# A decoder layer on one core: the products of the U tiles joined in pairs, VectorE adding the halves, table copies on ScalarE, 84 candidate sums

## What is computed

```
qry = (xt @ w_q).reshape(N, HEADS, 2, 128)
s = einsum('nhpd,pkd->nhpk', qry, sub_keys)         # 8 heads, 2 halves, 128 keys
s_top, i_top = top_k(s, 16)
cand = s_top[:, :, 0, :, None] + s_top[:, :, 1, None, :]    # 16 x 16 sums
cand_id = i_top[:, :, 0, :, None] * 128 + i_top[:, :, 1, None, :]
best, pos = top_k(cand, 16)
expert, gate = cand_id at pos, softmax(best)
hid = gelu(einsum('cd,chkd->chk', x, u_tab[expert]))
y = einsum('chk,chkd->cd', gate * hid, v_tab[expert])
```

## Time and profile before

| | |
|---|---|
| median of 3 runs | 1098.83 us (1098.72 to 1099.35) |
| the profiled execution's own time | 1099.08 us |
| its span, first to last instruction | 1097.3 us |
| mean granted TensorE clock | 0.997 |
| DVE, ACT, POOL busy | 70%, 51%, 16% of the span |

### The profile page before, as it was taken

How to read it: one execution, slowest core, us unless ns; L and a number is a source line. 1 busy time by engine, 2 the same in 40 slices (tenths; PEclk the granted TensorE clock), 3 DMA queues, 4 the chain that set the end, 5 groups by cost and what they waited for, 6 DMA issues and landing times.

```text
span 1097.3 us, 19861 instructions
## 1 busy us (share of the span) xinstructions
PE 1081.6 (99%) x6760; PEld 969.3 (88%) x6760; DVE 773.4 (70%) x1403; ACT 559.2 (51%) x903; POOL 177.5 (16%) x118
## 2 busy tenths in 40 slices
PE   8999999999999999999999999999999999999996
PEld 6888888678999999999999999998888888888885
DVE  4457657387999868889998777765555555555556
ACT  4347544564344555555556545545554455455553
POOL 2040002203000002223334555520000000000001
PEclk9999999999999999999999999999999999999998
DMA  7554344253445554444444443445565655555553
GB/s 280 190 194 155 134 157 150 96 173 129 159 166 180 185 179 155 156 163 160 153 154 153 142 146 134 137 153 193 198 208 204 205 193 191 191 191 191 192 193 112
DMA packets 52711, 186.48 MB, mean 170 GB/s; under 512 B 6320, under 2 KB 6704, under 8 KB 52672
## 3 DMA queue, kind: packets, MB, share of 16 engines
q1 hardware_dynamic: 50864, 181.30, 48.7%
q0 software_dynamic: 944, 3.15, 0.8%
q10 hardware_dynamic: 864, 1.57, 0.4%
HBM read 184.94 MB, written 1.05 MB: 169 GB/s over the span
## 4 chain that ended last, share of the span: by engine, by line
PE 92%; DVE 3%; DMA 2%; ACT 2%; POOL 1%; issue 1%; POOLq 0%; SPq 0%; DVEq 0%; ACTq 0%
PE ps L1172 17%; PE ps L1174 17%; PE ps L1173 17%; PE ps L1499 10%; PE ps L1500 10%; PE ps L1501 10%; PE ps L1460 5%; DMA raw<-w_tiles_in 1%; PE ps L1224 1%; ACT whi L462 1%; DVE wlo L726 1%; PE ps L1426 1%; PE ps L1300 1%; PE ps L1311 0%; PE ps L1316 0%
## 5 line engine op out<-in xcount | busy, mean ns | idle before, releaser
L726 DVE TENSOR_TENSOR wlo<-raw,whi 128x1024 fp32r<-128x1024 f32 x341 | 421.4, 1237 | 258.7 <-ACT whi L462 256.6
L462 ACT ACTIVATE whi<-raw 128x1024 fp32r<-128x1024 f32 x343 | 363.2, 1060 | 303.9 <-DMA raw<-w_tiles_v 167.8
L1172 PE MATMUL ps<-ahi,whi 128*128 128x256 f32 x1152 | 332.5, 289 | 0.4 <-DVE alo L987 0.4
L1174 PE MATMUL ps<-ahi,wlo 128*128 128x256 f32 x1152 | 325.8, 283 | 0.0
L1173 PE MATMUL ps<-alo,whi 128*128 128x256 f32 x1152 | 325.7, 283 | 0.0
L1172 PEld LDWEIGHTS ps<-ahi,whi 128*128 128x128 f32 x1152 | 220.6, 191 | 0.6 <-issue 0.6
L1173 PEld LDWEIGHTS ps<-alo,whi 128*128 128x128 f32 x1152 | 220.8, 192 | 0.0
L1174 PEld LDWEIGHTS ps<-ahi,wlo 128*128 128x128 f32 x1152 | 220.5, 191 | 0.0
L1499 PE MATMUL ps<-whi,hhi 128*128 128x512 f32 x512 | 199.3, 389 | 0.9 <-DVE wlo L726 0.9
L1500 PE MATMUL ps<-wlo,hhi 128*128 128x512 f32 x512 | 199.2, 389 | 0.0
L1501 PE MATMUL ps<-whi,hlo 128*128 128x512 f32 x512 | 199.2, 389 | 0.0
(11 more groups left out here) (198 smaller groups left out, 922.8 us busy)
## 6 DMA issues: line engine op xcount, KB each, us to landing
raw<-w_tiles_u SPq DMA_DIRECT2D x128, 512.0 KB, 3.2
raw<-w_tiles_v SPq DMA_DIRECT2D x128, 512.0 KB, 3.2
raw<-w_tiles_in SPq DMA_DIRECT2D x63, 512.0 KB, 3.2
raw<-w_tiles_q SPq DMA_DIRECT2D x16, 512.0 KB, 3.2
raw<-w_tiles_out SPq DMA_DIRECT2D x8, 512.0 KB, 3.2
xraw<-xT ACTq DMA_DIRECT2D x4, 256.0 KB, 6.3
xt<-x POOLq DMA_DIRECT2D x1, 1024.0 KB, 7.8
raw<-w_tiles_in SPq DMA_DIRECT2D x2, 256.0 KB, 4.6
```

Of the source, the lines that this page charges most:

```text
L462: act.activation(whi[:, tile.slot, :], raw[:, tile.slot, :], ACT.Copy)\
L726: dve.tensor_tensor(wlo[:, tile.slot, :], raw[:, tile.slot, :], whi[:, tile.slot, :].bitcast(F32), ALU.subtract)\
L1172: pe.matmul(out, ah, bh, start=start, stop=False)
L1174: return pe.matmul(out, al, bh, start=False, stop=stop)
```

## The change

- `ahi` and `alo` become two views of one tensor `pair`, in which high and low activations of a slice lie side by side. In U tiles 1 to 127 `by_pairs` takes the place of `by_tokens`: one product of 512 columns (high weights times high and low activations) and one of 256 columns (low weights times high activations, added to the second half of the bank). A tile has 16 products in place of 24, and the hidden values are the sum of the two halves of a bank.
- ACT copies the second half of the bank to SBUF (`low`), DVE adds it to the first half in PSUM (`add_low`), and ACT's gelu waits for that sum (`summed`). The late tokens' gelu is written back to PSUM, which takes the place of `gelu_late`. A bank is given back to PE at `merged`, from tile 38 on, in place of `hid_used`.
- The copy of a table to rows of `H` moves from DVE to ACT (`copy_g`, behind `split_hi`), and `into_h` keeps the multiplication, one iteration later. `hots` stands before `merge`, `widen_i` before gelu.
- `routing` makes 84 candidate sums in place of 256: rank a of one half meets only the first 16, 8 or 4 ranks of the other (`PAIR_ROWS`). The step that takes positions apart becomes two, with eight small operations more. Small tensors of the routing lie in unused rows of `H`.

```diff
+    pair = place("pair", [P, KC, 2, SEQ], F32R)
+    ahi, alo = pair[:, :, 0, :], pair[:, :, 1, :]
...
+        def copy_g(c):
+            there = after(c) + 1
+            act.wait_ge(S["g_done"], c + 1)
+            act.activation(H[:, there:NK, c * BLK:(c + 1) * BLK], tables(c)[:, there:NK, :], ACT.Copy)\
+                .then_inc(S["g_copied"], 1)
...
             act.wait_ge(S["tiles_used"], T_U + u + 1)
+            if u > 0:
+                if u > NTMP:
+                    act.wait_ge(S["summed"], u - NTMP)
+                act.activation(low[:, u % NTMP, :], ps[:, HID[u % 4], SEQ:2 * SEQ], ACT.Copy).then_inc(S["low_ready"], 1)
+            c = CHUNK_AFTER.get(u + 1)
+            if c is not None:
+                widen_i(c)
+            if u > 0:
+                act.wait_ge(S["summed"], u)
             if late > 0:
-                if u - FIRST_LATE >= NTMP:
-                    act.wait_ge(S["merged"], u - FIRST_LATE - NTMP + 1)
-                last = act.activation(gelu_late[:, u % NTMP, 0:late], ps[:, HID[u % 4], 0:late], ACT.Gelu)
+                last = act.activation(ps[:, HID[u % 4], 0:late], ps[:, HID[u % 4], 0:late], ACT.Gelu)
             if late < SEQ:
                 last = act.activation(H[:, u, late:SEQ], ps[:, HID[u % 4], late:SEQ], ACT.Gelu)
             last.then_inc(S["hid_used"], 1)
-            c = CHUNK_AFTER.get(u + 1)
-            if c is not None:
-                widen_i(c)
             split_hi(Tile(T_U + u + AHEAD))
+            c = CHUNK_AFTER.get(u)
+            if c is not None:
+                copy_g(c)
...
-                own.do(dve.tensor_tensor(cand[:, :, :], top[:, 0, :, None].to_broadcast([P, TOPK, TOPK]),
-                                         top[:, 1, None, :].to_broadcast([P, TOPK, TOPK]), ALU.add))
+                for first, end, width in PAIR_ROWS:
...
+                    own.step(dve.tensor_tensor(pairs, top[:, 0, first:end, None].to_broadcast([P, rows, width]),
+                                               top[:, 1, None, 0:width].to_broadcast([P, rows, width]), ALU.add))
...
+        def add_low(u):
+            hidden = ps[:, HID[u % 4], 0:SEQ]
+            dve.wait_ge(S["low_ready"], u)
+            dve.tensor_tensor(hidden, hidden, low[:, u % NTMP, :], ALU.add).then_inc(S["summed"], 1)
...
         for u in range(TILES_U):
+            if u > 0:
+                add_low(u)
+            c = CHUNK_AFTER.get(u + 2)
+            if c is not None:
+                hots(c)
             if u >= FIRST_LATE:
                 merge(u)
-            c = CHUNK_AFTER.get(u)
+            c = CHUNK_AFTER.get(u - 1)
             if c is not None:
                 into_h(c)
...
+        def by_pairs(tile, bank):
+            tile_ready(tile)
+            for k in range(KC):
+                cols = slice(k * P, (k + 1) * P)
+                pe.matmul(ps[:, bank, :], whi[:, tile.slot, cols], pair[:, k, :, :].rearrange("p a n -> p (a n)"),
+                          start=k == 0, stop=False)
+                last = pe.matmul(ps[:, bank, SEQ:2 * SEQ], wlo[:, tile.slot, cols], ahi[:, k, :], start=False,
+                                 stop=k == KC - 1)
+            last.then_inc(S["tiles_used"], 1)
```

More of the change, by code:

```diff
@@ L43 @@
 PH, NK, TOPK = 8, 128, 16
+PAIR_ROWS = ((0, 1, 16), (1, 3, 8), (3, 16, 4))
+PAIRS = sum((end - first) * width for first, end, width in PAIR_ROWS)
 ALPHA = 2.0 ** 0.25
@@ L277, in layer @@
     iota16 = place("iota16", [P, TOPK], BF16)
[L278 to L281, removed]
+    low = place("low", [P, NTMP, SEQ])
+    cand = place("cand", [P, PAIRS], alias=work_at + 99 * row + row // 2)
+    top = place("top", [P, 2, TOPK], alias=work_at + 99 * row + row // 2 + 352)
+    hot16 = place("hot16", [P, 4, 2, 2 * P], BF16, alias=work_at + 100 * row)
+    rank = place("rank", [P, 2, 2, 2, P], BF16, alias=work_at + 100 * row)
     gsum = place("gsum", [P, PH])
@@ L291, in layer, with tables @@
     HID = (2, 3, 4, 5)
+    def tables(c):
+        return ps[:, RING[c % 2], :].rearrange("p (n i) -> p i n", i=NK)
     Y_BANKS = (4, 5, 2, 3)
@@ L673, in _ @@
             last.then_inc(S["hid_used"], 1)
-            c = CHUNK_AFTER.get(u + 1)
+            split_hi(Tile(T_U + u + AHEAD))
+            c = CHUNK_AFTER.get(u)
             if c is not None:
-                widen_i(c)
-            split_hi(Tile(T_U + u + AHEAD))
+                copy_g(c)
             for t in range(NT):
@@ L1021, in routing @@
                     own.step(dve_idx(ids[:, a, 8:16], top[:, a, 8:16], s[a]))
-                own.do(dve.tensor_tensor(cand[:, :, :], top[:, 0, :, None].to_broadcast([P, TOPK, TOPK]),
-                                         top[:, 1, None, :].to_broadcast([P, TOPK, TOPK]), ALU.add))
+                at_pair = 0
+                for first, end, width in PAIR_ROWS:
+                    rows = end - first
+                    pairs = cand[:, at_pair:at_pair + rows * width].rearrange("p (a b) -> p a b", b=width)
+                    own.step(dve.tensor_tensor(pairs, top[:, 0, first:end, None].to_broadcast([P, rows, width]),
+                                               top[:, 1, None, 0:width].to_broadcast([P, rows, width]), ALU.add))
+                    at_pair += rows * width
+                own.wait()
                 yield
@@ L1034, in routing @@
             own.step(dve.tensor_copy(topf[:, 1, :].rearrange("p (q n) -> p q n", q=2), topi[:, :, 1, :]))
-            own.step(dve.tensor_scalar(posab[:, 0, 1, :], which, 4, None, ALU.logical_shift_right))
-            own.do(dve.tensor_scalar(posab[:, 1, 1, :], which, TOPK - 1, None, ALU.bitwise_and))
-            own.step(dve.tensor_copy(posf[:, 1, :].rearrange("p (a n) -> p a n", a=2), posab[:, :, 1, :]))
+            own.step(dve.tensor_scalar(posab[:, 0, 1, :], which, 2, None, ALU.logical_shift_right))
+            own.do(dve.tensor_scalar(posab[:, 1, 1, :], which, P - 1, None, ALU.bitwise_and))
+            own.do(dve.tensor_copy(posf[:, 1, :].rearrange("p (a n) -> p a n", a=2), posab[:, :, 1, :]))
+            yield
+            unit, place_in = posf[:, 1, 0:P], posf[:, 1, P:2 * P]
+            past4, past, over, twice = (rank[:, n // 2, 1, n % 2, :] for n in range(4))
+            own.step(dve.tensor_scalar(past4, unit, 4.0, None, ALU.is_ge))
+            own.do(dve.tensor_scalar(over, unit, 8.0, 0.0, ALU.subtract, ALU.max))
+            own.do(dve.scalar_tensor_tensor(out=past, in0=unit, scalar=6.0, in1=past4, op0=ALU.is_ge, op1=ALU.add))
+            own.do(dve.scalar_tensor_tensor(out=past, in0=unit, scalar=8.0, in1=past, op0=ALU.is_ge, op1=ALU.add))
+            own.step(dve.tensor_tensor(unit, past, over, ALU.add))
+            own.do(dve.tensor_tensor(twice, past, past4, ALU.add))
+            own.do(dve.scalar_tensor_tensor(out=twice, in0=twice, scalar=2.0, in1=over, op0=ALU.mult, op1=ALU.add))
+            own.do(dve.scalar_tensor_tensor(out=place_in, in0=twice, scalar=-4.0, in1=place_in, op0=ALU.mult,
+                                            op1=ALU.add))
             own.do(dve.tensor_tensor(gdiff[:, 1, :].rearrange("p (h k) -> p h k", k=TOPK), vals,
@@ L1474, in _ @@
         for k in range(1, 4):
-            by_tokens(Tile(T_U + k), HID[k])
+            by_pairs(Tile(T_U + k), HID[k])
         hidden(4, SEL_AT[0] + 1)
@@ L1478, in _ @@
         hidden(SEL_AT[0] + 1, ONE_PER_TWO)
-        for k in range(4):
+        for k in range(8):
             m = ONE_PER_TWO + k
-            pe.wait_ge(S["hid_used"], m - 3)
-            by_tokens(Tile(T_U + m), HID[k])
+            if m >= FIRST_LATE + 4:
+                pe.wait_ge(S["merged"], m - 3 - FIRST_LATE)
+            else:
+                pe.wait_ge(S["hid_used"], m - 3)
+            by_pairs(Tile(T_U + m), HID[k % 4])
             if k == 0:
```

45 lines of the change are left out of this document (22 added, 23 removed).

## The result

The changed kernel takes 1175.87 us (median of 6 runs, 1175.51 to 1177.1), the kernel before, run beside it, 1099.01. The ratio is 1.070, with a 95% interval of 1.069 to 1.071: slower by 77 us. The forecast was 1169 us, within 1148 to 1198.

A forecast was written before the change was run, and what follows sets the result against it. The prediction took PE's spacing in the U tiles to bound the kernel before, and a serial DVE-ACT loop the changed one: +32.5 + 8.5 + 33.0 - 4.3 = +69.7 on 1099.1 gives 1169 us, range 1148 to 1198.

The forecast's parts named there:

- The closed round: U tiles: sum, gelu, `split_hi`, `split_lo`, routing step and next sum run serially through DVE and ACT; chance 0.69.
- Its length: One round through DVE and ACT without a routing step: 2.96 us, or 3.01 with gelu in two pieces, above PE's 2.77.
- the mis-sized term: Tiles 34 to 87: rounds, routing steps, exponential and gates take 212.5 us against 179.5 before, +33.0.
- comparison steps beside POOL's multiplications as a danger: Rival of a longer loop: slow PSUM operations or stretched comparison steps; 0.3 us more a round gives 1194, 0.5 gives 1211; chance 0.12.
- The routing steps: DVE steps now paid inside the round: head steps 0.90 us in the mean, comparison steps 1.15, two decoding steps about 2.9.
- `hots`, `merge`, `into_h`, the copies at nothing: Tiles 34 to 87: these table operations cost nothing; uncovered, the first three would add up to a microsecond a tile.
- the cover that the prediction named: DVE's waiting time beside gelu and `split_hi`, 0.03 + 0.33 + 1.05 us; `copy_g` on ACT lies beside `split_lo` and the step.
- PE's saving: Joined products in U tiles: 2.773 us a tile, 0.107 less, 13.5 us over 127 tiles if PE stays the bound.
- stage four: Tiles 88 to 127, without routing steps: PE is the bound, 40 x -0.107 = -4.3 us.
- The rival "overlap": DVE and ACT overlap in the U tiles, only amount of work counts, PE stays the bound: 1085.6 us; chance 0.04.
- By stages: Forecast split of the U tiles: 1 to 24 +32.5, 25 to 33 +8.5, 34 to 87 +33.0, 88 to 127 -4.3.
- The rival "clock": PE idles in U tiles and its clock falls to 1.2 GHz; half of 84 tiles so, +55, about 1225 us; chance 0.06.

The follow-up runs named there:

- experiment 1: The changed kernel with `split_hi` of tile u+3 moved ahead of ScalarE's wait for the sum and gelu: 1103.32 us, ratio 1.003.
- experiment 2: The kernel before with one wait added: gelu of tile u waits for a count VectorE raises at the start of iteration u; 1171.99 us, ratio 1.066.
- experiment 6: The changed kernel with 256 candidate sums and the short decoding of places of the kernel before: 1183.41 us, ratio 1.077.
- Experiment 7: The changed kernel with the table copies back on VectorE, in its wait for gelu, and gone from ScalarE: 1177.13 us, ratio 1.071.
- experiment 10: The changed kernel with one wait added, so POOL's multiplication for a table starts only after the `split_lo` that follows `hots`: 1179.19 us, ratio 1.073.
- experiment 4: The changed kernel with the 512-column product split into two of 256 again, 24 products a tile: 1179.20 us, ratio 1.072.
- experiment 8: The changed kernel with four extra unused products of 256 columns in each of tiles 1 to 87: 1175.93 us, ratio 1.070.

## Why the prediction was right, step by step

- **The closed round** was the step that decided, and it holds three ways: the waits name each member of the circle, breaking it by one moved call gives back 73 of 77 us (experiment 1), and building it alone into the kernel before costs 72 (experiment 2).
- **Its length**: forecast 2.96 us without tables and 3.01 with. Measured without tables: 2.97. Measured in tiles 34 to 87: 3.03 in even tiles (handover 0.03 to 0.04 for 0.03, `split_hi` 1.06 for 1.05, the sum 0.43 for 0.42, `split_lo` 1.14 for 1.15) and 3.16 in odd ones. This is the mis-sized term, 33.0 forecast and 39.0 measured: 54 x 0.02 + 27 x 0.13 = 4.6 of the 6.0 us. The rest is small: exponential, `gates` and copies 3.2 for 2.7, steps 47.6 for 47.3, and PE starts tile 88 1.0 us later behind its `split_lo` than it does tile 34. The 0.13 come from `split_lo` beside POOL. I took its 1.15 from a tile of the kernel before in which POOL did not start first, though I had named comparison steps beside POOL's multiplications as a danger. The right danger stood at the wrong instruction.
- **The routing steps** in the round held: 84 sums save 7.5 us there (experiment 6), and tiles 1 to 24 came out at +33.4 for +32.5. In tiles 25 to 33 the changed kernel took 35.2 us as forecast (35.3); the 1.0 us that the difference is off lies in the kernel before, 27.7 for 26.8, where the transposes on PE behind tile 27 had been left out.
- **`hots`, `merge`, `into_h`, the copies at nothing**: right, under the cover that the prediction named. Experiment 7 shows it for the copies, and for the rest the rounds of experiment 10, which take 3.03 us whichever of these operations they hold. But the cover hid a wait of `merge` for gelu, which became the bound as soon as the first circle was open. I should have looked for the next circle before I put a range on experiment 1.
- **PE's saving**: -0.107 us a tile forecast, -0.08 measured (-3.3 us in stage four, 3.3 in experiment 4). From tile 88 on two of three tiles take 3.67 us, and the third 3.71, at 0.353 a pair of products rather than 0.347. Why every third tile is slower stays open; it coincides with nothing I could name, and was not tested. The Trainium skill's 2.5 ns beside the columns ("TensorE: Matmul & The Clock Gate", back-to-back issue gap), which it gives for an isolated product and not for a stream with weight loads like this one, would give 0.02 us a tile, 0.8 us over the stage. The runs give four times that.
- **The rival "overlap"** had the right amount of work: with both orders changed and the steps spread the kernel reaches 1091.93, though not the 1085.6 of a PE that never waits. By stages, 0.107 a tile would give -2.6, -1.0, -5.8 and -4.3, against the measured -0.2, -0.6, -3.5 and -3.4; the 6 us are spread over all of them, and what they are beyond the slower third tiles stays open.
- **The rival "clock"**: the granted clock did fall, in six stretches, and cost nothing (experiment 8). The prediction had counted it as a rival to the round; it only counts if PE's slower tile is longer than the round.

## What to carry to other kernels

Draw the waits of one iteration across the engines before adding one. If a chain leaves an engine and comes back to it within the same iteration, the sum of its members is the pace, and what stands on that chain in program order, however free before, is paid in full (here the routing steps). Only what fits under a wait of the round stays free (here the operations on tables). Then the order inside the iteration is worth more than any operation: issue what the other engine needs next first, and put the work that waits for the other engine last.

## What was not expected of the hardware

- DVE and POOL hold each other up. POOL's multiplication takes 1.97 us beside `split_lo` and 1.05 alone, a comparison on DVE 1.93 and 1.21, `split_lo` 1.35 and 1.23. The Trainium skill ("SBUF — State Buffer", SBUF: two separate sides) says that the two share a pair of ports as an exclusive lock, that a DVE operation with two SBUF inputs takes part in it against a POOL operation that reads SBUF, and that the later one blocks fully. The first two numbers fit: 545.34 to the end of `split_lo` at about 546.3, then 1.0 us of work. The third fits in direction only: the multiplication ran on for 0.26 us after `split_lo` had started, and cost it 0.12.
- In the kernel before, POOL's multiplication took 1.97 us on the mean, in the changed kernel 1.05, on the same data: its order, not its work, had been the price. Before, it started under `split_lo` (480.80 behind 480.64); in the changed kernel it is nearly through when `split_lo` starts.
- The granted clock was 0.86 on the mean over 388 to 418 us, at its lower level (1.2 GHz) for a part of it, after tiles before which PE mostly idled 0.8 to 1.9 us. With four more products in each tile it was 1.00 over the same stretch.
